# Loading the Hyena filter weights during the mixer's projection, and moving the first key tiles of cross-attention to other accumulators

## The reference, cut to what matters

```python
# Hyena: the long filters of each layer
hdn = jnp.sin(fr * (hdn @ w3 + b3))
filt = (hdn @ wout).reshape(l, HY_DIRS, HY_ORDER, HY_WIDTH)
filt = filt * jnp.exp(-t * deltas)[:, None, None, :]      # the fading
...
zz = gate * (_fft_conv(zz, kspec[:, o]) + skip[o] * zz)
# cross-attention: q from the tokens, k and v from the normed memory
kv = mem_n @ w_kv
```

## Time and profile before

| | us |
|---|---|
| median of three runs | 3937.5 |
| lowest and highest run | 3935.04, 3942.67 |
| the profiled execution | 3942.75 |
| its span in the trace | 3940.9 |
| mean granted clock of TensorE, share of full speed | 0.982 |

### The profile page before, as it was taken

One profiled execution on the slowest core, in us unless ns is written; L12 is line 12 of the kernel. 1 busy time (PEld: TensorE's weight loads), 2 busy tenths in 40 slices (PEclk: granted clock), 3 DMA queues, 4 the chain that ended last, 5 costly groups with the idle time before them and its releaser, 6 DMA issues. The chain is left out here.

```text
span 3940.9 us, 49851 instructions
## 1 busy us (share of the span) xinstructions
PE 3819.3 (97%) x19260; PEld 3131.9 (79%) x19260; DVE 2493.3 (63%) x3312; ACT 1512.6 (38%) x2113; POOL 334.2 (8%) x211
## 2 busy tenths in 40 slices
PE   8999999999999999999999999999999999999998
PEld 7988864988988898785597898866877888877886
DVE  6765756657674766565766776576647753547753
ACT  4342421443342433342243433355334542335531
POOL 2410000001320330000000241010000000000000
PEclk9999989999999999999999999999999999999999
DMA  3223220002322322321001222211312222222222
GB/s 129 98 92 109 84 78 1 1 22 107 106 87 94 107 102 85 108 86 54 1 1 65 107 96 91 105 32 44 128 65 86 96 91 101 107 71 90 96 91 80
DMA packets 53599, 314.81 MB, mean 80 GB/s; under 512 B 6735, under 2 KB 7569, under 8 KB 25557
## 3 DMA queue, kind: packets, MB, share of 16 engines
q1 hardware_dynamic: 53460, 312.94, 22.6%
HBM read 308.65 MB, written 2.10 MB: 79 GB/s over the span
## 5 line engine op out<-in xcount | busy, mean ns | idle before, releaser
L145 PE MATMUL bank<-hidden_hi,w_hi 128*128 128x512 f32 (+1 forms) x2400 | 910.5, 379 | 18.0 <-DVEq L363 6.6
L146 PE MATMUL bank<-hidden_lo,w_hi 128*128 128x512 f32 (+1 forms) x2400 | 906.3, 378 | 0.0
L147 PE MATMUL bank<-hidden_hi,w_lo 128*128 128x512 f32 (+1 forms) x2400 | 906.2, 378 | 0.0
L275 DVE TENSOR_TENSOR w_lo<-w_raw,w_hi 128x2048 fp32r<-128x2048 f32 (+1 forms) x240 | 485.7, 2024 | 380.1 <-ACT w_hi L270 375.0
L270 ACT ACTIVATE w_hi<-w_raw 128x2048 fp32r<-128x2048 f32 (+1 forms) x238 | 403.1, 1694 | 566.0 <-PE bank L147 527.6
L145 PEld LDWEIGHTS bank<-hidden_hi,w_hi 128*128 128x128 f32 x2400 | 453.7, 189 | 116.8 <-DVEq L262 16.1
L147 PEld LDWEIGHTS bank<-hidden_hi,w_lo 128*128 128x128 f32 x2400 | 453.3, 189 | 83.6
L146 PEld LDWEIGHTS bank<-hidden_lo,w_hi 128*128 128x128 f32 x2400 | 453.8, 189 | 82.5 <-issue 0.2
L145 PE MATMUL bank<-ffn_act_hi,w_hi 128*128 128x512 f32 x704 | 273.9, 389 | 0.0
L146 PE MATMUL bank<-ffn_act_lo,w_hi 128*128 128x512 f32 x704 | 273.9, 389 | 0.0
L147 PE MATMUL bank<-ffn_act_hi,w_lo 128*128 128x512 f32 x704 | 273.9, 389 | 0.0
(11 more groups left out here) (513 smaller groups left out, 7295.0 us busy)
## 6 DMA issues: line engine op xcount, KB each, us to landing
w_raw<-in_w_gu SPq DMA_DIRECT2D x131, 1024.0 KB, 4.7
w_raw<-in_w_down SPq DMA_DIRECT2D x96, 704.0 KB, 4.0
w_raw<-in_w_in SPq DMA_DIRECT2D x28, 1024.0 KB, 4.7
w_raw<-in_w_xattn SPq DMA_DIRECT2D x24, 1024.0 KB, 4.8
w_raw<-in_w_out SPq DMA_DIRECT2D x8, 1024.0 KB, 6.4
w_raw<-in_w_xattn_o SPq DMA_DIRECT2D x8, 1024.0 KB, 4.7
hyena_dft<-in_c_dft SPq DMA_DIRECT2D x6, 1024.0 KB, 9.5
w_raw<-in_w_qkv SPq DMA_DIRECT2D x6, 1024.0 KB, 4.8
```

The costliest lines, as they stand in the source:

```text
L145: nc.tensor.matmul(out, w_hi, x_hi, start=start, stop=False)
L146: nc.tensor.matmul(out, w_hi, x_lo, start=False, stop=False)
L147: return nc.tensor.matmul(out, w_lo, x_hi, start=False, stop=stop)
L275: nc.vector.tensor_tensor(self.lo[:, slot, 0:width], self.raw[:, slot, 0:width], self.hi[:, slot, 0:width].bitcast(F32), ALU.subtract)\
```

## The change

In the mixer's projection the SP stream now ends with the loads of `w` and `fade`. They go into `w_raw`: `w` to slot 0 once its last piece is split (`w_split0` at 7), `fade` in one transfer of 1 MB to slot 1 once that one is (`w_split1` at 7). SP waits for all five before the block ends. The Hyena stage uses both where they lie, its SP stream begins with the skip row and goes on with the table, PE alone waits for the skip, and DVE no longer waits for any load. In cross-attention the first slot of turn 4 uses banks 4 and 5 instead of 0 and 1 and waits for two moves of values; turn 5's first slot waits for all four.

```diff
@@ cross_attention
+            def tile_bank(turn, slot, j):
+                return m.bank[4 + j if turn == 4 and slot == 0 else 2 * slot + j]
@@ tiles
-                        last = product3(nc, m.bank[2 * slot + j][:, 0:n], w_hi, w_lo, *x_tiles(k),
+                        last = product3(nc, tile_bank(turn, slot, j)[:, 0:n], w_hi, w_lo, *x_tiles(k),
@@ PE, before the keys
-                pe.wait_ge(S.sem("v_out"), 2 * MT)
+                pe.wait_ge(S.sem("v_out"), MT)
                 for turn in range(4, 6):
                     for slot in range(2):
                         if turn > 4:
-                            pe.wait_ge(S.sem(f"moved{slot}"), 6)
+                            pe.wait_ge(*(S.sem("moved1"), 6) if slot else (S.sem("v_out"), 2 * MT))
@@ ACT's moves read tile_bank(turn, slot, j) in the same way
@@ mixer_in, SP
             ring.loads(sp, S, io["w_in"], first + 2, 6, 1)
+            w, fade = taps
+            sp.wait_ge(S.sem("w_split0"), 7)
+            for dst, src in ((w[0:HID, 0, :], io["hy_f_wout"][L][0]), (w[HID:P, 0, :], io["hy_f_wout"][L][1]),
+                             (w[0:HID, 1, :], io["hy_f_wout"][L][0]), (w[HID:P, 1, :], io["c_back"])):
+                sp.dma_start(dst, src).then_inc(S.sem("taps_loaded"), 16)
+            sp.wait_ge(S.sem("w_split1"), 7)
+            sp.dma_start(fade[:, :, :], io["c_fade"]).then_inc(S.sem("taps_loaded"), 16)
+            sp.wait_ge(S.sem("taps_loaded"), 80)
@@ hyena, SP
-            for dst, src in ((w[0:HID, 0, :], io["hy_f_wout"][L][0]), (w[HID:P, 0, :], io["hy_f_wout"][L][1]),
-                             (w[0:HID, 1, :], io["hy_f_wout"][L][0]), (w[HID:P, 1, :], io["c_back"]),
-                             (skip[:, :], io["hy_skip"][L])):
-                sp.dma_start(dst, src).then_inc(S.sem("w_loaded"), 16)
-            for t in range(TT):
-                sp.dma_start(fade[:, t, :], io["c_fade"][:, t]).then_inc(S.sem(f"fade{t}"), 16)
+            sp.dma_start(skip[:, :], io["hy_skip"][L]).then_inc(S.sem("skip_loaded"), 16)
@@ hyena, PE
             pe.wait_ge(S.sem("w_ready"), 1)
+            pe.wait_ge(S.sem("skip_loaded"), 16)
@@ hyena, DVE
-            dve.wait_ge(S.sem("w_loaded"), 80)
...
-                dve.wait_ge(S.sem(f"fade{t}"), 16)
```

More of the change, by code:

```diff
@@ L1615, in move @@
                             act.wait_ge(S.sem(f"tiles{slot}"), 2 * count + j + 1)
-                            nc.scalar.activation(dst[:, 4 * (turn % 2) + 2 * slot + j, :], m.bank[2 * slot + j][:, 0:n],
+                            nc.scalar.activation(dst[:, 4 * (turn % 2) + 2 * slot + j, :], tile_bank(turn, slot, j)[:, 0:n],
                                                  ACT.Copy).then_inc(S.sem(f"moved{slot}"), 1)
@@ L1962, with mixer_in @@
 SINES = (16, 20, 24)
-def mixer_in(nc, m, early, io, L, qkv_t, z_t, hy_t, fold, hid, gates):
+def mixer_in(nc, m, early, io, L, qkv_t, z_t, hy_t, fold, hid, gates, taps):
     first = L * 14
@@ L2380, in first_turn, with hyena @@
     return v
-def hyena(nc, m, io, L, hy_t, fold, hid, turn0):
+def hyena(nc, m, io, L, hy_t, fold, hid, taps_from, turn0):
     with Stage(nc, f"hyena{L}", settle=True) as S:
@@ L2393, in hyena @@
         spec, spec_at = placed("spec", [P, ORDERS, 2, TT, HY])
-        fade, fade_at = placed("fade", [P, TT, HY])
-        w, w_at = placed("w", [P, 2, ORDERS * HY])
-        assert nc.sbuf_base <= SBUF_TOP
+        w, fade = taps_from
+        w_at, fade_at = m.w_raw_at, m.w_raw_at + UNIT * 4
+        assert nc.sbuf_base <= m.w_raw_at
         def view(at, n, width):
@@ L3364, in persistent @@
     m.w_raw = top("w_raw", [P, 2, UNIT])
+    m.w_raw_at = at
     m.w_lo = top("w_lo", [P, 2, UNIT], F32R)
@@ L3563, in mixer @@
             made = delta_places(nc, m, L)
-            mixer_in(nc, m, early, io, L, qkv_t, z_t, hy_t, fold, m.sq, gates)
-            hy_rows = hyena(nc, m, io, L, hy_t, fold, m.sq, first_turn(nc, m, gates, made, qkv_t))
+            taps = (nc.alloc_sbuf_tensor_at(f"mix{L}_taps_w", [P, 2, ORDERS * HY], F32, offset=m.w_raw_at),
+                    nc.alloc_sbuf_tensor_at(f"mix{L}_fade", [P, TT, HY], F32, offset=m.w_raw_at + UNIT * 4))
+            mixer_in(nc, m, early, io, L, qkv_t, z_t, hy_t, fold, m.sq, gates, taps)
+            hy_rows = hyena(nc, m, io, L, hy_t, fold, m.sq, taps, first_turn(nc, m, gates, made, qkv_t))
         delta_rule(nc, m, L, z_t, qkv_t, hy_rows, gates, made, out_early)
```

## The result

The changed kernel takes 3912.22 us (median of four runs, 3910.74 to 3913.98) beside 3936.27 for the kernel before (four runs): ratio 0.9929, interval 0.9917 to 0.9941. Later sets of five runs gave 3910.86 beside 3938.44 (0.9929, 0.9914 to 0.9944) and 3908.64 beside 3941.11 (0.9911, 0.9898 to 0.9925). So the change saves 24 to 32 us, 0.6 to 0.9%. By the medians the first set's gain of 24.1 us is inside it. The measured ratio, which is not the quotient of the two medians (0.9939), stands for 28 us and lies just beyond it; its interval takes in both.

A forecast was written before the change was run, and what follows sets the result against it. PE, busy for 97% of the span, was taken as the bound. Hyena's 12.1 us and cross-attention's 8.9 made 21.0, giving 3921.7 from the profiled 3942.75 and 3916.5 from the median; forecast 3920 us, range 3911 to 3932.

The forecast's parts named there:

- What bounds it: Whole kernel: PE, busy for 97% of the span, sets the time; its two touched waits make 11.4 us.
- The next late things: After the waits: PE's turning in the first Hyena stage, ACT's moves in the second, no new wait in cross-attention.
- The cover of the moved loads: Mixer's projection: SP has the loads at about 541, the next stage starts at 555.1, some 14 us of cover.
- Only changes its name: Rival in cross-attention: PE stops for the weights' split instead; 8.9 us lost at most, 3925 to 3929, chance 0.06.
- slower: Rival at the projection's end: the five loads land late and every engine waits, twice; 3945 and more, chance 0.02.
- Waits, 11.0 us: Idle time of PE removed: 1.8 and 3.3 us before the Hyena taps, 5.9 us in both key projections.
- The collision, 0.5 per stage: Hyena stage start: DVE's two passes meet POOL's backward copy and delay it, a cost of 0.5 us per stage.
- my second rival: Hyena: both DVE passes push back POOL's copy, PE's third tile 1.9 us later; 3927 to 3932, chance 0.12.
- The clock in the taps: Hyena taps: one lower-clock fall of 3.4 us left per stage, so gains of 4.9 and 3.1 us.
- My first rival: The waits go but the low clock stays: a gain of 10.0 us, 3927.5 to 3932.8, chance 0.22.
- The clock in the keys: Key projections: without the idleness before them the clock's fall goes, 1.5 us gained in each.
- the anchor: Starting time for the gain: 3920 chosen between 3921.7 (from the profiled execution) and 3916.5 (from the median).

The follow-up runs named there:

- full rows: The change with the skip product over 128 rows (127 of them zeros) instead of one: 3907.02 us, and 3904.94 us in a later set.
- run 7: The change with POOL's backward copy made to wait for DVE's two passes: 3912.82 us beside 3939.71 for the kernel before.
- run 5: The change with the skip product over 128 rows instead of one: 3907.02 us beside 3939.71 for the kernel before, ratio 0.9917.
- run 6: The kernel before, all its waits kept, with the skip product over 128 rows instead of one: 3922.05 us, ratio 0.9958.
- 9: The change with DVE's two passes before the taps waiting for the table's second 1 MB: 3925.97 us beside 3940.09, ratio 0.9964.
- 10: The change with the skip product over 128 rows and DVE's two passes waiting for the table's second 1 MB: 3919.05 us, ratio 0.995.
- the cross half: The kernel before with only the change's cross-attention part put in: 3930.17 us beside 3938.44, ratio 0.9972.

## Why the prediction was right or wrong

**What bounds it** was right: PE lost its two waits, and the gain is time of PE. **The next late things** were named rightly in all four places: turning in the first Hyena stage, ACT's moves in the second (0.50 us left), nothing in the key projections. The cover of the moved loads held. "Only changes its name" and "slower" did not happen.

**Waits, 11.0 us**: measured at 1.8 and 3.2 us less idleness before the taps and 5.9 in the keys. Right.

**The collision, 0.5 per stage**: 0. POOL's copy kept its 1.89 us and DVE took the whole delay, 1.22 to 2.95. The Trainium skill's exclusive lock for whoever issues first (SBUF — State Buffer, Who interferes with whom) fits: the copy started 0.02 us earlier, and DVE's pass ended 1.1 us after it. It fits with full rows too, where DVE zeroes `skip` first: there its pass starts 1.2 us later, takes 1.77 us, and again ends 1.1 us after the copy in all four stages. With DVE first, run 7, the order was forced by a semaphore, so it shows the price of the order (PE's 2.69 us), not the lock. Run 7 is also my second rival, tried: with its clock it ends at 26.9 us less than before, so it was mis-priced as well as wrong.

**The clock in the taps**, one fall of 3.4 us left per stage: right, in all ten stages of the five traces that have the change's Hyena code as it is, and the two profiles differ in the taps by 4.8 and 3.2 us, beside my 4.9 and 3.1. The reason was half right. I had put the falls down to idleness and skips and could not say how they share; runs 5, 6, 9 and 10 show that they act together, with the reserve on the idle times above. My first rival, that the low clock stays, was wrong, and so is the rule of the skill taken alone (TensorE: Matmul & The Clock Gate, What's actually happening) where it goes by a busy PE: a PE that the trace shows as busy, with single-row products, is not spared. The trace models the ends of products, so the pauses of 0.19 us count as busy in it.

**The clock in the keys**, 1.5 us each: 4.74 - 2.97 = 1.8 measured. But the sum stopped at the end of the projection. **The step that failed** is "the 2.97 us of idleness is the only thing in front of the fall of the clock there; without it I give back half of about 3.2 us per projection": there was a second fall, in the scores, in all eight stages with the wait and in 2 of 20 without. It was in the trace of before, at 2887.1 and 3481.1 us, and I never listed the clock behind the stage. That is 3.4 us.

**The second step that failed** is the anchor: "If its excess was falls of the clock of the kind that I count, the median holds fewer of them to win". Nothing shows its excess in the touched places. It reached the first Hyena stage at 555.1 us, the thirteen other traces between 550.3 and 553.7, so some 3 of its 5.25 us lay ahead of every removed wait. From stage start to the first spectra it needed 34.6 and 32.8 us, the cross half's trace, with the same Hyena code, 32.9 and 37.0; from the last value product to the scores it is 28.9 us in all eight stages with the wait. So the anchor cost 3.5 us (3920 instead of 3916.5).

The sum of 21.0, plus 1.0 for no collision and 3.4 for the scores, is 25.4; off the median of three that is 3912.1, against 3912.22 measured. That they meet so closely is luck: the three sets differ by 8 us. The Hyena part was too small as well, and that is the sum's third gap. The mean from start to first spectra, 34.3 us over the four stages with the old code and 26.9 over the ten with the new, gives 14.8 rather than my 12.1; with the 12.9 above that is 27.7 us, near the middle of the three sets. The old code's four stages range from 32.8 to 37.0, so this mean is loose. The price of taps at the higher clock, 18.9, was 0.2 too high: run 7 has them at 18.7 without a fall.

## What to carry to other kernels

Price a removed wait with the clock behind it, not only up to the end of the stage: here the waits were 11 us and the clock about 16. The part in the scores rests on its going with the wait, not on a known link. Where one profiled execution is above the median, look where its excess lies before any is taken off the gain. And a bias that is added by a product with a single row is worth a look: over 128 rows, mostly zeros, it took 17.7 us off the kernel before (run 6); on top of the change its 4 us or so are not clear of noise.

## What the runs showed of the hardware that I had not expected

- A single-row float32 product between full ones cost 1.05 us per product at 2.4 GHz, and so did its neighbour; with 128 rows the next product starts after 0.86. That is eight products by 0.19, 1.5 us per stage (18.7 us in run 7, 17.2 in run 5), with the same number of columns.
- The granted clock fell, or stayed down, while the trace had PE busy with taps and single-row products: 10 to 17 us at 1.2 GHz in all five stages where it had idled 3.6 to 4.0 us before them, 10 us and a second fall of 3.4 in one of three where it had idled 1.7 to 1.9, and 3.4 us in the ten stages of the change. With full rows, and 2.8 to 3.5 us of idleness, no stretch was longer than 3.4 us.
- A wait of 3 us in the projection was followed in 8 of 8 stages by a fall of 3.4 us in the keys, about 1 us after PE went on, and by another in the scores, 35 us later. Without the wait the first came in none of 20 stages, the second in 2.
- Two engines released together by one barrier met in the same order each time: in all ten stages of the five traces with the change's Hyena code POOL's copy took 1.89 us and DVE's pass 2.95, its own 1.22 and 1.73 more.
